# Order of the three products of a split matmul: the lower activation streams first

## The reference

```python
# first_block
f1 = swiglu(rms_norm(h, g), w_gate, w_up, w_down)       # 1024 -> 2816 -> 1024
h = h + 0.5 * rms_norm(f1, g_post)
proj = rms_norm(h, g) @ w_in                            # latent, dilated and gate projections
merged = gates[0] * (o_a @ w_branch_a) + gates[1] * (o_b @ w_branch_b)
h = h + rms_norm(merged @ w_out, g_post)
h = h + 0.5 * rms_norm(swiglu(rms_norm(h, g), w_gate, w_up, w_down), g_post)
# second_block
u = modulate(rmsnorm(x, g), shift, scale) @ w_in        # mLSTM, attention and SSD inputs, gates
x = x + mod * ((g_m * (y_m @ w_m) + g_a * (y_a @ w_a) + g_s * (y_s @ w_s)) @ w_out)
x = x + mod * conv_ffn(modulate(rmsnorm(x, g), shift, scale), w_up, conv_w, w_down)
```

## The kernel before

| place | upper weight | lower weight | upper activation | lower activation |
|---|---|---|---|---|
| three feed-forward layers | 48 | 0 | 32 | 0 |
| projections, output products | 48 | 0 | 32 | 0 |
| first two tiles of the second output product (`branch_uppers` with `late_parts`) | 0 | 0 | 32 | 0 |
| three branches of the second block (`branch_parts`) | 0 | 0 | 48 | 48 |
| `stay_awake`, one operand for both | 32 | | 32 | |

## Time and profile before

### The profile page before, as it was taken

The page is one execution under the profiler, slowest core; times in us unless marked ns, Lnnn a source line. Parts: engine busy times, 40 slices in busy tenths (PEclk is TensorE's granted clock), DMA queues, the critical chain, the costliest instruction groups (busy, mean ns, idle before and its releaser), DMA issues.

```text
span 1206.9 us, 24404 instructions
## 1 busy us (share of the span) xinstructions
PE 1178.4 (98%) x9128; PEld 1111.1 (92%) x9128; DVE 816.0 (68%) x1121; ACT 637.3 (53%) x1018; POOL 527.1 (44%) x285
## 2 busy tenths in 40 slices
PE   6999999999999999999999999999999999999998
PEld 6999999987889899999999879987877999999998
DVE  7788875856865577777654852688836596655555
ACT  6444446525762555454546546468517635655553
POOL 0343436732465533343436645458530483232331
PEclk9999998999999999999989999999999999999999
DMA  6888884543334467878614333233323254666663
GB/s 221 277 278 294 283 280 130 190 140 123 105 108 137 157 210 259 292 274 292 188 52 158 123 99 129 88 106 105 105 70 106 88 175 140 208 185 188 188 189 121
DMA packets 58100, 207.10 MB, mean 172 GB/s; under 512 B 6576, under 2 KB 8240, under 8 KB 57776
## 3 DMA queue, kind: packets, MB, share of 16 engines
q1 hardware_dynamic: 49824, 177.23, 45.2%
q0 software_dynamic: 6912, 25.17, 5.7%
q10 hardware_dynamic: 1296, 3.74, 0.9%
HBM read 205.07 MB, written 1.05 MB: 171 GB/s over the span
## 4 chain that ended last, share of the span: by engine, by line
PE 82%; DVE 8%; issue 3%; ACT 3%; POOL 2%; DMA 1%; DVEq 0%; SPq 0%; POOLq 0%; ACTq 0%
PE psum L641 23%; PE psum L642 23%; PE psum L643 22%; POOL own_parts L2944 2%; PE psum L789 1%; PE psum L1017 1%; PE psum L942 1%; PE psum L652 1%; PE psum L654 1%; PE psum L653 1%; PE psum L666 1%; PE psum L1346 1%; POOL high L3039 1%; DVE u_parts L2882 1%; PE psum L700 1%
## 5 line engine op out<-in xcount | busy, mean ns | idle before, releaser
L641 PE MATMUL psum<-parts 128*128 128x256 f32 x1584 | 441.0, 278 | 14.0 <-DVE parts L2197 10.4
L642 PE MATMUL psum<-parts 128*128 128x256 f32 x1584 | 445.7, 281 | 0.0
L643 PE MATMUL psum<-parts 128*128 128x256 f32 x1584 | 441.6, 279 | 0.0
L641 PEld LDWEIGHTS psum<-parts 128*128 128x128 f32 x1584 | 299.5, 189 | 14.9 <-issue 11.0
L2952 POOL TENSOR_TENSOR parts<-low,parts 128x1024 fp32r<-128x1024 f32 x60 | 151.0, 2517 | 367.4 <-ACT parts L1520 367.4
L643 PEld LDWEIGHTS psum<-parts 128*128 128x128 f32 x1584 | 299.7, 189 | 0.0
L642 PEld LDWEIGHTS psum<-parts 128*128 128x128 f32 x1584 | 299.7, 189 | 0.0
L1520 ACT ACTIVATE parts<-low 128x1024 fp32r<-128x1024 f32 x198 | 207.4, 1056 | 163.1 <-DMA low<-stream 162.4
L2944 POOL TENSOR_TENSOR own_parts<-low,parts 128x1024 fp32r<-128x1024 f32 x75 | 184.9, 2479 | 151.5 <-ACT parts L1598 147.4
L2197 DVE TENSOR_TENSOR parts<-low,parts 128x1024 fp32r<-128x1024 f32 x138 | 163.6, 1219 | 23.6 <-ACT parts L1520 22.9
L642 PE MATMUL psum<-u_parts,parts 128*128 128x256 f32 (+1 forms) x560 | 164.7, 294 | 0.0
(11 more groups left out here) (384 smaller groups left out, 2091.1 us busy)
## 6 DMA issues: line engine op xcount, KB each, us to landing
low<-stream SPq DMA_DIRECT2D x334, 512.0 KB, 3.6
high<-conditioning POOLq DMA_DIRECT2D x48, 512.0 KB, 5.0
high<-wuq ACTq DMA_DIRECT2D x1, 1152.0 KB, 5.1
low<-x SPq DMA_DIRECT2D x4, 256.0 KB, 6.3
high<-ctx ACTq DMA_DIRECT2D x1, 1024.0 KB, 6.4
out<-low SPq DMA_DIRECT2D x8, 128.0 KB, 1.8
low<-cst ACTq DMA_DIRECT2D x1, 850.5 KB, 4.8
low<-vec ACTq DMA_DIRECT2D x1, 157.5 KB, 6.3
```

What stands on the lines that cost most here:

```text
L641: pe.matmul(out, w_hi[:, cols_], x_hi, start=start, stop=False, **kw)
L642: pe.matmul(out, w_hi[:, cols_], x_lo, start=False, stop=False, **kw)
L643: return pe.matmul(out, w_lo[:, cols_], x_hi, start=False, stop=stop, **kw)
```

## The change

The first two lines of `split_product` change places, with the flag that starts the accumulator. Each group of three now asks for upper weight by lower activation, upper weight by upper activation, lower weight by upper activation. Nothing else changes: the same operands in the same places, the same waits ahead of the group, the same signal behind it.

```diff
             def split_product(out, w, cols_, x, start, stop, **kw):
 
                 (w_hi, w_lo), (x_hi, x_lo) = w, x
-                pe.matmul(out, w_hi[:, cols_], x_hi, start=start, stop=False, **kw)
-                pe.matmul(out, w_hi[:, cols_], x_lo, start=False, stop=False, **kw)
+                pe.matmul(out, w_hi[:, cols_], x_lo, start=start, stop=False, **kw)
+                pe.matmul(out, w_hi[:, cols_], x_hi, start=False, stop=False, **kw)
                 return pe.matmul(out, w_lo[:, cols_], x_hi, start=False, stop=stop, **kw)
```

## The result

The changed kernel took 1221.4 us, the median of nine executions, against 1208.2 us, the median of nine of the kernel before (the three known ones among them). The ratio is 1.010, with a 95% interval of 1.0077 to 1.0123: slower by 12 us. The forecast was 6 us slower, 1211.5 us, and the measured median lies above the stated range (1197 to 1217). Of the 9.9 us between forecast and measurement, 2.7 are the base, since six more executions moved the median of the kernel before from 1205.5 to 1208.2; the rest is the change itself. The sign was right, the size was half, and two of the signs that the prediction named for its mechanism came out wrong: the third product did not read 277 ns, and the branches did not stay at 281.

The account below looks back on a forecast made before the run. TensorE's matmul start-to-start distance was taken as the bound: 117 + 118.5 + 114.5 = 350.0 ns a group against 346.5, by 2080 groups 7.3 us, rounded to 6. 1205.5 + 6 = 1211.5 us, range 1197 to 1217; slower had chance 0.48.

Parts of the forecast that it names:

- the third product did not read 277 ns: Sign in the feed-forward windows: the third product (L643) should last about 277 ns, with L641 at 279 or 280, L642 281.
- TensorE's start-to-start distance bounds the kernel, no wait moves, and every ns reaches the end.: Feed-forward layers: TensorE busy 50.00 of 50 us, nothing covers the cost; a group takes 346.5 ns before, 350.0 after.
- The time depends on where the streams start, not on the work.: Products of one shape last 276 to 283 ns, by start columns of what they read and of the weight loaded beside.
- Each product has the price of its own pair.: Streaming activation and weight loaded beside it set each product's time: 117, 118.5 and 114.5 ns after the change.
- The branches stay at 281: Branches' 96 groups: all pairs are (48, 0) under either order, so durations should still read 281 ns.
- The rounding from 7.3 down to 6 us: Whole kernel: 2080 groups by 3.5 ns is 7.3 us, rounded down because the first product's 117 ns was a choice.
- the same count of 2080 groups: Whole kernel: 2370 groups on the chain, less 96 of branches, 80 for 512-column groups, and a twentieth covered by DVE or POOL.
- No change: Rival for the whole kernel: the order is indifferent, same three prices, 1205.5 us; chance 0.27.
- Faster by the end of equal starts: Rival: products whose two streams start equal are dear; new order has none, 4 ns less a group, 1197 us; chance 0.25.
- The price of single operands: Mechanism of the no-change rival: loading a weight at 48 is cheap, one at 0 dear, whatever streams; 1205.5 us, chance 0.27.
- The rule on ports: Skill's rule of two independent SBUF read ports, cited for no change: which weight loads beside which activation changes nothing.

Follow-up runs that it names:

- new_in_ffn: New order in the three feed-forward layers alone, the old one elsewhere, against the kernel before: 1218.5 us, ratio 1.0076.
- turned_old: Old cycle begun at another product (lower weight by upper activation first), same places, against the kernel before: 1209.9 us, ratio 1.001, 346.7 ns a group.
- places_old: Old order, lower operands' start columns changed differently in each feed-forward layer (lower activation 0, lower weight 0, all equal_old's places), against the kernel before: ratio 1.0076.
- places_new: The three sets of start columns of places_old, under the new order, against the kernel before: ratio 1.0075.
- low16_new: New order everywhere; in the feed-forward layers lower weight at 16, both activations at 32; against the kernel before: 1205.6 us, ratio 0.994.
- equal_old: Old order; in the feed-forward layers lower weight moved to 48, lower activations to 32, like the upper ones; against the kernel before: 1215.2 us, ratio 1.004.
- new_outside_ffn: Old order in the feed-forward layers, new one in projections, branches and output products, against the kernel before: 1210.6 us, ratio 1.0012.
- low16_old: Old order everywhere; in the feed-forward layers lower weight at 16, both activations at 32; against the kernel before: 1204.4 us, ratio 0.995.

## Why the prediction was half right

- *TensorE's start-to-start distance bounds the kernel, no wait moves, and every ns reaches the end.* Right in the layers. Their growth is the sum of their groups' within 1 us, and new_in_ffn carries three quarters of the loss by itself. Outside them less came through than I counted.
- *The time depends on where the streams start, not on the work.* Right. turned_old keeps the pairs and the pace, places_old and places_new have, in their first two layers, the same pairs and the same pace under two orders, and low16_new shows that the new order is not slow in itself. That the weight loaded beside a product counts, and not only its own weight, follows from the change: each activation has the same weights of its own under both orders, and the pace differs.
- *Each product has the price of its own pair.* Wrong, and this is the step that failed. First and second product were estimated at 117 and 118.5 ns and measured at 117.5 or 118.3 and 118.3 or 119.2. The third was kept at 114.5 because its pair stayed, and measured 117.5 in one pace and 119.2 in the other. That is 3.0 of the 3.3 ns, or 4.7 of the 6.7, that were missing in a group of 350.0. That the first two came close is in part luck: 117 was a choice between 113.5 and 119, and 118.5 is a duration less 162.5. The steady state of a cycle belongs to the three pairs together. The two times that (32, 48) had before, 276 and 278 ns, were a sign of this that I averaged; and the third product of before was not one value "equal to the nanosecond", but 277 in one half of the groups and 278 in the other.
- *The branches stay at 281.* Wrong in one profile, right in the other: their pairs have two paces, 340.0 and 353.3 ns, and the last tiles of the branches are at the first in one profile of the changed kernel and at the second in the other. Nothing in the order did it, since equal_old has 340.0 there with untouched branches.
- *The rounding from 7.3 down to 6 us* went the wrong way. With 353.3 and 356.7 ns in place of 350.0, the same count of 2080 groups gives 14 to 21 us, more than was measured; so the count, too, was generous. The layers' 1584 groups account for 12.4 of the 12.8 us, and new_outside_ffn as a whole for 0.1%; of the 500 or so groups that the count had outside, little reached the end.
- *The rivals.* No change fell with the ratio. Faster by the end of equal starts fell with the changed kernel, which has none and is slower, and with places_old: under the old order, (0, 48) or (32, 0) in place of (0, 0) gave 353.3 and 354.7 ns for 346.7. The price of single operands fell with the third product, which kept both of its own.
- *The rule on ports.* By the Trainium skill's page TensorE: Matmul & The Clock Gate, part 2, the load of weights takes no read bandwidth from the running matmul. The pace does not follow from that: with the old order and nothing but the start of the lower weight changed, from 48 to 16, it went from 353.3 in all three layers of equal_old to 340.0 in all three of low16_old. Whether read bandwidth is what is lost, no run shows.

Left open is the mechanism below this: why some sets have one pace and others two, and what picks between two when TensorE starts again. The trace shows the choice and not its reason. Many different sets share the paces 340.0, 353.3, 356.7, 357.8 and 360.0 ns, others lie between them or above, and no run here tells why.

## What to carry to other kernels

In a dense stretch of matmuls with a weight load each, an order of products and the start columns of their operands belong together; a new order needs its places looked for anew, and its price can't be added up from the products of the old one. Count the matmuls in a window where nothing waits, in several stretches between late starts and in two executions at least, before a pace is called fixed; read distances from starts and not from durations. A test is cheap where the kernel has several like layers, since each can be given its own places in one run.

## What was not expected of the hardware

One program ran the same layer at 340.0 or 353.3 ns a group, 4% apart, with the granted clock at 1.00 in both, and changed from one to the other at a start that came 0.17 us late. Moving both activations by 4 columns (16 bytes), from a distance of 16 to one of 12 or 20, took a group from 340.0 or 353.3 ns to 357.5 or 357.8.
